# First modulation pieces: five of eight summed by VectorE, and four buffers with three pairs of banks for the rows of x

## The chip, the cores and the metric

One core of one Trainium2 chip. The metric is the device time of one execution in microseconds (us), as the median of several runs. All data are float32 unless said otherwise.

## The reference, cut to what matters

```python
c_act = silu(c)
mod = c_act @ ada_w + ada_b                    # (1, 1024) @ (1024, 6144)
sh1, sc1, g1, sh2, sc2, g2 = split(mod, 6)
h = rms_norm(x, mix_norm_g) * (1 + sc1) + sh1  # x: 512 x 1024
z = h @ w_in                                   # everything else starts from z
...                                            # two attention mixers, then a mixture of 64 experts
```

So the first product with `w_in` needs two things: x, scaled by its row's root and turned so that the 1024 features lie on the partitions, and for every feature its shift `sh1` and scale `sc1`. Those are 2048 of the 6144 columns of `mod`, each a sum over 1024 rows of `ada_w`.

## The kernel before

The 2048 columns are made in eight pieces of 256 columns, numbered 0 to 7. Piece 2p holds shifts and piece 2p+1 scales of the 256 features of pair p. A piece of `ada_w` is 1 MB: 128 partitions by 8 blocks k by 256 columns, in `AF[u]` (`AF[0]` to `AF[5]` in `R_Z`, `AF[6]` and `AF[7]` in `R_WT`). There are two ways to sum one:

- **TensorE** (`ada_quarters`, L1346): eight matrix products, block k against a column of `c_act` in `CQ`, each on a group of 32 rows of the array, so that four partial sums stand in a bank `QBANK[u]`. VectorE copies them to `ACC` (`ada_parts`, L922). Every matmul of float32 is two instructions in the profile, so one piece is 16 of L1346.
- **VectorE** (`ada_sum`, L886 and L888): one multiply and seven multiply-adds over 128 x 256, with partial sums for 128 partitions in `ACC`.

Either way TensorE then turns the partial sums into sums that lie on the partitions (`ada_by_feature`, L1330, two matmuls of one column, four instructions a piece), VectorE adds bias and gain (`mod_columns`, L913 and L915), ScalarE applies them to HT (`modulate`, L708), and TensorE multiplies (`project_first`, L1379).

`QUARTERS = [0, 1, 2, 3, 5, 7]` lists the pieces that TensorE sums; VectorE sums 4 and 6. The first two are summed ahead of the projection. `project_first` runs over k = 0 to 7, and in each k over the four row tiles t. After t = 1 of k = 1, 3, 5 it calls `ada_by_feature` for the two pieces of the next pair; after k = 0, 2, 4 it calls `ada_quarters` for those of the next two pieces that TensorE sums. k needs its half pair to be modulated (`s_hma`) and its quarter of the first weights (`s_w0`).

Ahead of that stand the rows of x. ScalarE makes the root of each of the four row tiles; VectorE scales a tile into `HROW[t % 2]` (`x_row`, L903); TensorE turns it in two halves of four transposes into banks 6 and 7 (`turn_row`, L1314); ScalarE takes bank 6 (L699) and VectorE bank 7 (`take_xt_first`, L907). The single pair of banks makes tile t wait for both copies of tile t-1, and the two buffers make `x_row` wait for transposes.

The work of each engine is written out by hand in one order. SyncE issues all loads in this order: c, gain and bias, constants, four tiles of x, pieces 0 and 1, first quarter of the weights, pieces 2 and 3, second quarter, 4 and 5, third quarter, 6 and 7, fourth quarter, further constants, a 32 KB load, 2 MB of the second weights. None of these waits for work of an engine other than the memsets at the start. Behind them piece 8 waits for seven finished sums (`s_acc`) and piece 9 for eight, since they use the buffers of pieces 6 and 7. ScalarE issues six small loads of 4 to 32 KB (QKG, bfg, rbias) right behind the first pair's `modulate`.

Of the kernel before, what the change touches and what calls it, by code (L numbers as in the profile page):

```python
# [25 lines left out]
P = 128  # L26
# [5 lines left out]
NT = S // P  # L32
# [12 lines left out]
HC = 256  # L45
# [58 lines left out]
    return sum(a in into for into in INTO[:n]) + (a == 0 and n > NM - TAIL)  # L104


QUARTERS = [0, 1, 2, 3, 5, 7]
QBANK = {0: 0, 1: 1, 2: 6, 3: 7, 5: 6, 7: 7}

NEG = -1e30  # L110
NOTOK = 1024.0
# [49 lines left out]
def build(nc, a):  # L161
    f32, i32, bf16 = mybir.dt.float32, mybir.dt.int32, mybir.dt.bfloat16
    ALU, ACT, AX = mybir.AluOpType, mybir.ActivationFunctionType, mybir.AxisListType

    st = contextlib.ExitStack()
    with st:
# [16 lines left out]
        R_G = sb("R_G", [P, 8192])  # L183
# [5 lines left out]
        X = R_XM[:, 0:4096].rearrange("p (t n) -> p t n", t=NT)  # L189
        MOD = R_XM[:, 4096:8192].rearrange("p (r n) -> p r n", r=4)  # L190
        HT = R_HT[:, :].rearrange("p (k s) -> p k s", k=KD)
# [4 lines left out]
        AF = [R_Z[:, 2048 * u:2048 * (u + 1)].rearrange("p (k n) -> p k n", k=KD) for u in range(6)]\  # L196
            + [AD[:, 0], AD[:, 1]]
        ROWS = R_A[0:32, 0:P]
        ACC = R_A[:, :].rearrange("p (b n) -> p b n", b=4)
        HROW = R_S[:, 0:2048].rearrange("p (b n) -> p b n", b=2)  # L200
        JUNK = R_S[:, 2048:3072]
        SQT = R_S[:, 0:2048].rearrange("p (t n) -> p t n", t=NT)
        GN = R_G[:, 0:1024]

# [25 lines left out]
        def tab(at):  # L230
# [22 lines left out]
        ssx = sb("ssx", [P, 12])  # L253
# [8 lines left out]
        CQ = R_S[:, 3072:3072 + 32 * KD].rearrange("p (k h) -> p k h", k=KD)  # L262
# [18 lines left out]
        PS = st.enter_context(nc.psum_tensor("PS", [P, 8, 512], f32))  # L281
# [10 lines left out]
        s_rowst, s_ada1, s_mcol, s_hma, s_htd = map(sem, (  # L292
            "rows_turned", "first_ada_done", "mod_columns_ready", "h_ready_act", "ht_ready_dve"))
# [6 lines left out]
        s_cact, s_acc, s_ones, s_madd, s_mod2 = map(sem, (  # L300
            "c_act_ready", "ada_sums_ready", "ada_spread", "mod_added", "mod2_ready"))
        s_ssx, s_hrow, s_xpose, s_ht = map(sem, ("x_root_ready", "h_row_ready", "h_transposed", "ht_ready"))
# [34 lines left out]
        s_aq = sem("ada_quarters_done")  # L337
# [8 lines left out]
        def need(eng, s, value):  # L346

            if isinstance(value, int) and value <= 0:
                return
            eng.wait_ge(s, value)  # L350
# [331 lines left out]
        def _(act):  # L682
# [13 lines left out]
                               bias=cst[:, C_SC:C_SC + 1]).then_inc(s_ssx, 1)  # L696
            for t in range(NT):
                act.wait_ge(s_xpose, 2 * t + 1)
                act.activation(HT[:, 0:4, P * t:P * t + P], PS[:, 6, :].rearrange("p (k s) -> p k s", k=4), ACT.Copy)\  # L699
                    .then_inc(s_ht, 1)  # L700
            act.sem_inc(s_zfree, 4)
            act.wait_ge(s_ht, NT)
# [91 lines left out]
            for n in range(8):  # L794
                t = n // 2
# [77 lines left out]
        def _(dve):  # L873
            link = Chain(dve, s_dch)

            def ada_sum(u):

                src = AF[u] if u < 8 else AD[:, u % 2]
                acc = ACC[:, u % 4]
                if u < 8:  # L880
                    dve.wait_ge(s_af[u], 16)
                    need(dve, s_ada1, u - 3)
                else:
                    dve.wait_ge(s_ada[u % 2], 16 * (u // 2 - 3))
                    need(dve, s_ones, u - 11)
                link(dve.tensor_scalar(acc, src[:, 0], cact[:, 0:1], None, ALU.mult))  # L886
                for k in range(1, KD):
                    ins = dve.scalar_tensor_tensor(acc, src[:, k], cact[:, k:k + 1], acc, ALU.mult, ALU.add)  # L888
                    if k < KD - 1:
                        link(ins)  # L890
                ins.then_inc(s_acc, 1)
# [6 lines left out]
            def x_row(t):  # L898
                dve.wait_ge(s_ssx, t + 1)
                link(dve.reciprocal(ssx[:, 8 + t:9 + t], ssx[:, 4 + t:5 + t]))  # L900
                if t >= 2:
                    dve.wait_ge(s_xpose, 2 * t - 2)
                dve.tensor_scalar(HROW[:, t % 2], X[:, t, :], ssx[:, 8 + t:9 + t], None, ALU.mult).then_inc(s_hrow, 1)  # L903

            def take_xt_first(t):
                dve.wait_ge(s_xpose, 2 * t + 2)
                dve.tensor_copy(HT[:, 4:8, P * t:P * t + P], PS[:, 7, :].rearrange("p (k s) -> p k s", k=4))\  # L907
                    .then_inc(s_htd, 1)

            def mod_columns(p):  # L910
# [6 lines left out]

            def ada_parts(u):

                dve.wait_ge(s_aq, QUARTERS.index(u) + 1)  # L920
                need(dve, s_ada1, u - 3)
                dve.tensor_copy(ACC[:, u % 4], PS[:, QBANK[u], 0:HC]).then_inc(s_acc, 1)  # L922

            x_row(0)
            x_row(1)
            take_xt_first(0)
            x_row(2)
            take_xt_first(1)
            x_row(3)
            take_xt_first(2)  # L930
            take_xt_first(3)
            for p in range(4):
                for u in (2 * p, 2 * p + 1):
                    if u in QUARTERS:
                        ada_parts(u)
                    else:
                        ada_sum(u)
                mod_columns(p)

            def log_forget():  # L940
# [116 lines left out]
            for n in range(8):  # L1057
                t, cols = n // 2, slice(512 * (n % 2), 512 * (n % 2) + 512)
# [16 lines left out]
            for n in range(8):  # L1075
                t, cols = n // 2, slice(512 * (n % 2), 512 * (n % 2) + 512)
# [220 lines left out]
        def _(pe):  # L1297
# [13 lines left out]
            def turn(dst_bank, src, ready):  # L1311

                for k in range(4):
                    ins = pe.transpose(PS[:, dst_bank, P * k:P * k + P], src[:, P * k:P * k + P], ident)  # L1314
                ins.then_inc(ready, 1)

            def turn_row(t):
                pe.wait_ge(s_hrow, t + 1)
                for half in range(2):
                    need(pe, s_htd if half else s_ht, t)  # L1320
                    turn(6 + half, HROW[:, t % 2, 512 * half:512 * half + 512], s_xpose)

            def ada_by_feature(u):

                p, r = u // 2, u % 2
                pe.wait_ge(s_acc, u + 1)
                need(pe, s_mcol, p - 1)
                for half in range(2):
                    n = 2 * r + half
                    ins = mm(PS[:, 4 + p % 2, n:n + 1], ACC[:, u % 4, P * half:P * half + P], ones[:, 0:1],  # L1330
                             start=True, stop=True)
                ins.then_inc(s_ada1, 1)

            def ada_quarters(u):

                pe.wait_ge(s_cact, 3)
                pe.wait_ge(s_af[u], 16)
                if u == 2:
                    pe.wait_ge(s_ht, NT)
                elif u == 3:  # L1340
                    pe.wait_ge(s_htd, NT)
                elif u > 3:
                    pe.wait_ge(s_acc, QUARTERS[QUARTERS.index(u) - 2] + 1)
                for k in range(KD):
                    g = k % 4
                    ins = mm(PS[32 * g:32 * g + 32, QBANK[u], 0:HC], CQ[:, k, :], AF[u][:, k, :], start=k < 4, stop=k >= 4)  # L1346
                ins.then_inc(s_aq, 1)

            for t in range(NT):
                turn_row(t)  # L1350
            for u in range(2):
                ada_quarters(u)
            for u in range(2):
                ada_by_feature(u)

# [419 lines left out]
```

## Time and profile before

| | |
|---|---|
| median of 3 runs | 1297.62 us (1295.75 to 1299.5) |
| the profiled execution | 1296.77 us, of which the span is 1294.9 us |
| TensorE busy | 1204.2 us, 93% of the span |
| VectorE busy | 462.3 us, 36% |
| mean granted clock of TensorE | 0.971 of full |

A span runs from the first instruction to the last. "Idle before" behind an instruction is the time its engine stood still before it, with the instruction or transfer that ended the wait. "Us to landing" of a load counts from the start of its issue to the arrival of its last byte. The change touches the first 51 us of the span only.

### The profile page before, as it was taken

What the parts mean: (1) busy time and instruction counts of PE and PEld (TensorE: products, weight loads), DVE (VectorE), ACT (ScalarE), POOL (GpSimd) and SP (SyncE); (2) the same over time, 40 slices, a digit from 0 to 9 for tenths busy, and PEclk for the clock granted to TensorE, in tenths of its full rate; (3) what the DMA queues carried; (4) which work ended last, traced back from release to release, by engine and by line L of the source; (5) the groups of instructions that cost most, each with busy time, mean ns of one, the idle gap of its engine ahead of it and who ended that gap; (6) DMA issues with size and microseconds to landing.
All of it is one profiled execution on the core that took longest, in us unless ns stands there. A gap on an engine that the chain in (4) does not pass through costs nothing.

```text
span 1294.9 us, 14018 instructions
## 1 busy us (share of the span) xinstructions
PE 1204.2 (93%) x4705; PEld 605.5 (47%) x4705; DVE 462.3 (36%) x1239; ACT 197.5 (15%) x452; POOL 193.2 (15%) x221
## 2 busy tenths in 40 slices
PE   6999999999999999996999998888999888999985
PEld 3444544444888544443444443333444343444442
DVE  2536557100666232554332333222323222233322
ACT  3210001011655001110010110000101010011100
POOL 0000000000220000100123222221222112213212
PEclk9999999999999999997999999888999899999998
DMA  8966661112000301257499999999989999989972
GB/s 278 369 207 227 221 225 65 65 65 105 27 0 1 130 30 83 91 228 306 170 333 372 387 361 378 367 360 372 366 279 381 385 363 387 384 267 378 360 218 35
DMA packets 87327, 311.51 MB, mean 241 GB/s; under 512 B 12225, under 2 KB 37985, under 8 KB 62049
## 3 DMA queue, kind: packets, MB, share of 16 engines
q1 hardware_dynamic: 71040, 272.77, 54.6%
q0 software_dynamic: 14784, 35.68, 11.8%
q10 hardware_dynamic: 1440, 2.27, 0.5%
q8 instruction: 35, 0.57, 0.2%
q14 instruction: 28, 0.22, 0.0%
HBM read 295.47 MB, written 34.08 MB: 254 GB/s over the span
## 4 chain that ended last, share of the span: by engine, by line
PE 73%; DMA 19%; DVE 2%; issue 2%; SPq 2%; ACT 1%; POOL 0%; DVEq 0%; POOLq 0%; ACTq 0%
PE PS L1396 19%; PE PS L1685 18%; DMA R_WT<-w_up_e 9%; PE PS L1706 9%; PE PS L1564 4%; PE PS L1535 4%; DMA R_XM<-w_up_e 3%; PE PS L1468 2%; PE PS L1379 2%; PE PS L1671 2%; PE PS L1444 2%; DMA out<-second_sum 2%; DMA R_Z<-w_up_e 2%; PE PS L1574 2%; PE PS L1456 1%
## 5 line engine op out<-in xcount | busy, mean ns | idle before, releaser
L1396 PE MATMUL PS<-R_WT,R_HT 128*128 128x512 f32 x576 | 248.2, 592 | 0.0
L1685 PE MATMUL PS<-R_Z,R_G 128*128 128x512 f32 (+1 forms) x496 | 202.6, 629 | 13.4 <-DMA R_Z<-w_up_e 10.1
L1396 PEld LDWEIGHTS PS<-R_WT,R_HT 128*128 128x128 f32 x576 | 109.3, 190 | 135.9 <-issue 135.8
L1232 DVE TENSOR_TENSOR R_G<-R_G,PS 128x256 f32<-128x256 f32 x50 | 30.5, 610 | 368.2 <-ACT R_G L836 368.2
L1685 PE MATMUL PS<-R_WT,R_G 128*64 128x512 f32 (+1 forms) x400 | 143.4, 623 | 17.0 <-DMA R_Z<-w_up_e 12.1
L1685 PEld LDWEIGHTS PS<-R_Z,R_G 128*128 128x128 f32 (+1 forms) x496 | 75.6, 173 | 111.4 <-issue 111.4
L628 POOL DMA_INDIRECT R_G<-h_rows,gidx x54 | 56.2, 1040 | 446.4 <-DVE gidx L1221 367.4
L841 ACT ACTIVATE R_G<-PS 128x256 f32<-128x256 f32 x50 | 19.2, 384 | 571.5 <-PE PS L1693 555.5
L1685 PE MATMUL PS<-R_XM,R_G 128*128 128x512 f32 (+1 forms) x208 | 95.6, 614 | 8.3 <-DMA R_WT<-w_up_e 8.3
L1706 PE MATMUL PS<-R_Z,R_G 128*128 128x512 f32 (+1 forms) x248 | 99.7, 603 | 0.8 <-issue 0.8
L1253 DVE SCALAR_TENSOR_TENSOR R_G<-PS,slx,R_XM 128x512 f32<-128x512 f32 x100 | 75.0, 751 | 61.8 <-PE PS L1706 61.8
L1685 PEld LDWEIGHTS PS<-R_WT,R_G 128*64 128x64 f32 (+1 forms) x400 | 52.1, 161 | 93.4 <-issue 93.4
L634 POOL DMA_INDIRECT out<-R_G,ridx x38 | 55.9, 1470 | 104.4 <-DVE R_G L1253 57.1
L1706 PE MATMUL PS<-R_WT,R_G 128*64 128x512 f32 (+1 forms) x200 | 69.6, 599 | 0.0
L1671 PE MATMUL PS<-cst,R_G 128*128 128x128 f32 x416 | 56.7, 282 | 13.2 <-DMA R_G<-h_rows,gidx 13.2
L1008 DVE CUSTOM_DVE_ANT_0 R_S<-PS,R_A 128x128 f32<-128x128 f32 (+1 forms) x64 | 28.9, 489 | 106.5 <-PE PS L1444 106.4
L888 DVE SCALAR_TENSOR_TENSOR R_A<-R_WT,cact,R_A 128x256 f32<-128x256 f32 x119 | 57.7, 485 | 4.3
L1685 PEld LDWEIGHTS PS<-R_XM,R_G 128*128 128x128 f32 (+1 forms) x208 | 35.0, 170 | 50.0 <-issue 50.0
L1671 PEld LDWEIGHTS PS<-cst,R_G 128*128 128x128 f32 x416 | 49.1, 146 | 14.7 <-DMA R_G<-h_rows,gidx 14.7
L1564 PE MATMUL PS<-R_Z,R_HT 128*128 128x512 f32 x128 | 55.4, 592 | 0.0
L1535 PE MATMUL PS<-R_WT 128*128 128x512 f32 x128 | 55.4, 592 | 0.0
L1706 PEld LDWEIGHTS PS<-R_Z,R_G 128*128 128x128 f32 (+1 forms) x248 | 35.1, 165 | 38.7 <-issue 38.6
(250 smaller groups left out, 1239.1 us busy)
## 6 DMA issues: line engine op xcount, KB each, us to landing
R_Z<-w_gate_e SPq DMA_DIRECT2D x26, 1024.0 KB, 13.9
R_Z<-w_up_e SPq DMA_DIRECT2D x26, 1024.0 KB, 21.8
R_Z<-w_down_e SPq DMA_DIRECT2D x26, 1024.0 KB, 17.0
R_WT<-w_gate_e SPq DMA_DIRECT2D x25, 1024.0 KB, 14.8
R_WT<-w_up_e SPq DMA_DIRECT2D x25, 1024.0 KB, 23.0
R_WT<-w_down_e SPq DMA_DIRECT2D x25, 1024.0 KB, 19.6
R_WT<-ada_w SPq DMA_DIRECT2D x18, 1024.0 KB, 7.5
R_WT<-w_in SPq DMA_DIRECT2D x9, 2048.0 KB, 10.3
```

Source lines behind the costliest of these rows:

```text
L628: pool.indirect_dma_start(out=XG[0:rows(j), b, :], out_offset=None, in_=h2_dram, in_offset=bass.IndirectOffsetOnAxis(ap=gidx[b][0:rows(j), ...
L634: pool.indirect_dma_start(out=sum_dram if n else a["out"], out_offset=bass.IndirectOffsetOnAxis(ap=index[0:part.shape[0], 0:1], axis=0), i ...
L888: ins = dve.scalar_tensor_tensor(acc, src[:, k], cact[:, k:k + 1], acc, ALU.mult, ALU.add)
L1008: ins = dve.tensor_tensor_reduce(out=PB[:, b, at:at + w], in0=PS[:, g, src:src + w], in1=TB[:, b, S - w:S], scale=1.0, scalar=-3e38, op0=A ...
L1232: dve.tensor_tensor(AR[:, b, :].rearrange("p (k d) -> p d k", k=2), by_line(SIL[:, b, :], 2), by_line(PS[:, b, F:2 * F], 2), ALU.mult).the ...
L1253: dve.scalar_tensor_tensor(OB[:, b, 512 * half:512 * half + 512], PS[:, 2 + half, :], slx[:, bass.ds(j % 8, 1), 2:3].rearrange("p o c -> p ...
L1396: ins = mm(PS[:, t, :], HT[:, k, P * t:P * t + P], WR[:, b, k, :], start=k == 0, stop=k == KD - 1)
L1535: ins = mm(PS[:, 2 * half + r, :], YT[:, 4 * r + k, P * t:P * t + P], w[:, k, 512 * half:512 * half + 512], start=k == 0, stop=k == 3)
L1564: ins = mm(PS[:, n % 4, :], MT[:, k, P * t:P * t + P], WO[:, k, 512 * half:512 * half + 512], start=k == 0, stop=k == KD - 1)
L1671: ins = pe.transpose(PS[:, 4 + half, P * k:P * k + P], XG[:, b, 512 * half + P * k:512 * half + P * k + P], ident)
L1685: ins = mm(PS[w * h:w * h + w, b, :].rearrange("p (g n) -> p g n", g=2), XT[:, b, k, w * h:w * h + w], WGU[n][:, k], start=k == 0, stop=k ...
L1706: ins = mm(PS[w * h:w * h + w, 2 + half, :], AT[:, b, k, w * h:w * h + w], WDN[n][:, k, 512 * half:512 * half + 512], start=k == 0, stop=k ...
```

## The change

TensorE sums pieces 0, 1 and 2; VectorE sums 3 to 7. Pieces 0 and 1 share bank 5, in columns 0 to 255 and 256 to 511; piece 2 uses bank 6. The rows of x get four buffers `XROW[t]` and the pairs of banks (6,7), (0,1), (2,3), (6,7). TensorE turns tiles 0 to 2, sums pieces 0 and 1, then turns tile 3, which alone waits for a copy. VectorE sums piece 3 ahead of its copy of piece 2. No load is added, removed or moved in SyncE's order.

```diff
-QUARTERS = [0, 1, 2, 3, 5, 7]
-QBANK = {0: 0, 1: 1, 2: 6, 3: 7, 5: 6, 7: 7}
+QUARTERS = [0, 1, 2]
+QBANK = {0: 5, 1: 5, 2: 6}
+QCOL = {0: 0, 1: HC, 2: 0}
+XBANK = (6, 0, 2, 6)
...
+        XROW = R_G[:, 2048:6144].rearrange("p (b n) -> p b n", b=NT)
...
             def x_row(t):
                 dve.wait_ge(s_ssx, t + 1)
                 link(dve.reciprocal(ssx[:, 8 + t:9 + t], ssx[:, 4 + t:5 + t]))
-                if t >= 2:
-                    dve.wait_ge(s_xpose, 2 * t - 2)
-                dve.tensor_scalar(HROW[:, t % 2], X[:, t, :], ssx[:, 8 + t:9 + t], None, ALU.mult).then_inc(s_hrow, 1)
+                dve.tensor_scalar(XROW[:, t], X[:, t, :], ssx[:, 8 + t:9 + t], None, ALU.mult).then_inc(s_hrow, 1)
...
             def ada_parts(u):
 
-                dve.wait_ge(s_aq, QUARTERS.index(u) + 1)
-                need(dve, s_ada1, u - 3)
-                dve.tensor_copy(ACC[:, u % 4], PS[:, QBANK[u], 0:HC]).then_inc(s_acc, 1)
+                dve.wait_ge(s_aq, max(2, u + 1))
+                dve.tensor_copy(ACC[:, u % 4], PS[:, QBANK[u], QCOL[u]:QCOL[u] + HC]).then_inc(s_acc, 1)
 
             x_row(0)
             x_row(1)
             take_xt_first(0)
             x_row(2)
+            x_row(3)
             take_xt_first(1)
-            x_row(3)
             take_xt_first(2)
+            ada_parts(0)
+            ada_parts(1)
             take_xt_first(3)
-            for p in range(4):
-                for u in (2 * p, 2 * p + 1):
-                    if u in QUARTERS:
-                        ada_parts(u)
-                    else:
-                        ada_sum(u)
+            mod_columns(0)
+            ada_sum(3)
+            ada_parts(2)
+            mod_columns(1)
+            for p in range(2, 4):
+                ada_sum(2 * p)
+                ada_sum(2 * p + 1)
                 mod_columns(p)
...
             def turn_row(t):
                 pe.wait_ge(s_hrow, t + 1)
                 for half in range(2):
-                    need(pe, s_htd if half else s_ht, t)
-                    turn(6 + half, HROW[:, t % 2, 512 * half:512 * half + 512], s_xpose)
+                    if t == 3:
+                        pe.wait_ge(s_htd if half else s_ht, 1)
+                    turn(XBANK[t] + half, XROW[:, t, 512 * half:512 * half + 512], s_xpose)
...
-                pe.wait_ge(s_acc, u + 1)
+                pe.wait_ge(s_acc, 4 if u == 2 else u + 1)
...
-            for t in range(NT):
+            for t in range(3):
                 turn_row(t)
             for u in range(2):
                 ada_quarters(u)
+            turn_row(3)
             for u in range(2):
                 ada_by_feature(u)
```

## Rows read from the trace of the kernel before

**Rows 1.** The page, part 4: shares of the chain that ended last.

```profile
PE 73%; DMA 19%; DVE 2%; issue 2%; SPq 2%; ACT 1%; POOL 0%; DVEq 0%; POOLq 0%; ACTq 0%
```

**Rows 2.** Chain of the first 110 us: start us, us, what.

```profile
18.41 1.86 PE PS L1346 x32
...
28.27 1.86 PE PS L1346 x32
...
32.84 5.26 PE PS L1379 x12
38.09 1.00 PE PS L1346 x16
...
41.01 0.79 PE PS L1330 x8
...
50.75 8.69 PE PS L1379 x20
```

**Rows 3.** Timeline of TensorE, 9 to 30 us: start, us, instructions, idle before.

```profile
13.13 5.28 PE L1314 MATMUL PS<-cst,R_S 128*128 128x128 f32 x24 [1.65 <-DVE R_S L903]
...
22.90 5.37 PE L1379 MATMUL PS<-R_WT,R_HT 128*128 128x512 f32 x8 [1.48 <-ACT R_HT L708]
```

**Rows 4.** Timeline of VectorE: bias and gain of a pair, then sums of pieces 8, 9.

```profile
21.47 0.16 DVE L913 TENSOR_TENSOR mcol<-PS,gcol 128x4 f32<-128x4 f32 x1 [0.70 <-PE PS L1330]
...
56.37 0.35 DVE L886 TENSOR_SCALAR R_A<-R_WT,cact 128x256 f32<-128x256 f32 x1 [5.22 <-DMA R_WT<-ada_w]
...
60.28 0.35 DVE L886 TENSOR_SCALAR R_A<-R_WT,cact 128x256 f32<-128x256 f32 x1
60.67 3.61 DVE L888 SCALAR_TENSOR_TENSOR R_A<-R_WT,cact,R_A 128x256 f32<-128x256 f32 x7
```

**Rows 5.** Timeline of SyncE, issue of pieces 1, 3, 4, 5, 6, 7: start, us.

```profile
5.04 1.35 SPq L460 DMA_DIRECT2D R_Z<-ada_w  x1
...
11.69 2.92 SPq L460 DMA_DIRECT2D R_Z<-ada_w  x1
...
18.18 0.71 SPq L460 DMA_DIRECT2D R_Z<-ada_w  x1
...
18.93 2.92 SPq L460 DMA_DIRECT2D R_Z<-ada_w  x1
...
25.43 2.63 SPq L460 DMA_DIRECT2D R_WT<-ada_w  x1
...
28.11 6.68 SPq L460 DMA_DIRECT2D R_WT<-ada_w  x1
```

**Rows 6.** DMA view at those six issues, same order: KB, us to landing.

```profile
R_Z<-ada_w SPq DMA_DIRECT2D x1, 1024.0 KB, 11.6
...
R_Z<-ada_w SPq DMA_DIRECT2D x1, 1024.0 KB, 12.4
...
R_Z<-ada_w SPq DMA_DIRECT2D x1, 1024.0 KB, 14.0
...
R_Z<-ada_w SPq DMA_DIRECT2D x1, 1024.0 KB, 17.8
...
R_WT<-ada_w SPq DMA_DIRECT2D x1, 1024.0 KB, 16.4
...
R_WT<-ada_w SPq DMA_DIRECT2D x1, 1024.0 KB, 16.7
```

**Rows 7.** DMA view of 27 to 33 us.

```profile
DMA packets 1066, 0.65 MB, mean 109 GB/s; under 512 B 514, under 2 KB 1066, under 8 KB 1066
```

**Rows 8.** Windows: stretch, length, busy (instructions) of PE, PEld, DVE, ACT, POOL; clock; DMA; GB/s.

```profile
24.10:27.50 3.40, 3.40 (x5) 1.35 (x4) 0.00 (x0) 0.00 (x0) 0.00 (x0) 0.51 1.07 327
```

**Rows 9.** Windows of TensorE alone, expert stage: length, busy (instructions), clock, DMA, GB/s.

```profile
640.00:644.00 4.00, 2.95 (x12) 1.00 0.51 205
...
708.00:712.00 4.00, 4.00 (x15) 0.72 1.03 391
```

**Rows 10.** Timeline of TensorE at 706 us.

```profile
706.44 0.69 PE L1685 MATMUL PS<-R_WT,R_G 128*64 128x512 f32 x1 [2.33 <-DMA R_Z<-w_up_e]
```

More of the change, by code:

```diff
@@ L698, in _ @@
                 act.wait_ge(s_xpose, 2 * t + 1)
-                act.activation(HT[:, 0:4, P * t:P * t + P], PS[:, 6, :].rearrange("p (k s) -> p k s", k=4), ACT.Copy)\
+                act.activation(HT[:, 0:4, P * t:P * t + P], PS[:, XBANK[t], :].rearrange("p (k s) -> p k s", k=4), ACT.Copy)\
                     .then_inc(s_ht, 1)
@@ L900, in x_row @@
                 link(dve.reciprocal(ssx[:, 8 + t:9 + t], ssx[:, 4 + t:5 + t]))
-                if t >= 2:
-                    dve.wait_ge(s_xpose, 2 * t - 2)
-                dve.tensor_scalar(HROW[:, t % 2], X[:, t, :], ssx[:, 8 + t:9 + t], None, ALU.mult).then_inc(s_hrow, 1)
+                dve.tensor_scalar(XROW[:, t], X[:, t, :], ssx[:, 8 + t:9 + t], None, ALU.mult).then_inc(s_hrow, 1)
             def take_xt_first(t):
                 dve.wait_ge(s_xpose, 2 * t + 2)
-                dve.tensor_copy(HT[:, 4:8, P * t:P * t + P], PS[:, 7, :].rearrange("p (k s) -> p k s", k=4))\
+                dve.tensor_copy(HT[:, 4:8, P * t:P * t + P], PS[:, XBANK[t] + 1, :].rearrange("p (k s) -> p k s", k=4))\
                     .then_inc(s_htd, 1)
@@ L1339, in ada_quarters @@
                     pe.wait_ge(s_ht, NT)
[L1340 to L1343, printed above, removed]
                 for k in range(KD):
                     g = k % 4
-                    ins = mm(PS[32 * g:32 * g + 32, QBANK[u], 0:HC], CQ[:, k, :], AF[u][:, k, :], start=k < 4, stop=k >= 4)
+                    ins = mm(PS[32 * g:32 * g + 32, QBANK[u], QCOL[u]:QCOL[u] + HC], CQ[:, k, :], AF[u][:, k, :], start=k < 4, stop=k >= 4)
                 ins.then_inc(s_aq, 1)
-            for t in range(NT):
+            for t in range(3):
                 turn_row(t)
```

## The prediction

> **What bounds the kernel now.** I read the page first: the chain that ended last is TensorE for 73% and transfers for 19% [rows 1]. The transfers belong to the experts' weights, long after the changed part, so the question is what stands in the chain of the first 51 us [rows 2]. The reader is to see there that TensorE works without a gap from 22.90 us on, and that three stretches of the partial sums on TensorE are links of it: 1.86 us for pieces 2 and 3, then 1.00 us for piece 5 and the same again for piece 7. Behind 51 us TensorE goes on into the second weights, so a shift of the end of the last columns (50.75 us, where the projection resumes) passes on one to one, and everything up to there can be reckoned as one time. The third view is the timeline of TensorE [rows 3]: 24 transposes of x take 5.28 us with their waits, and the projection starts at 22.90 us after 1.48 us of standing still. The fourth, and the one that decides here, is when the pieces land [rows 5, 6], read as start of the issue plus time to landing:
>
> - piece 1: 5.04 + 11.6 = 16.6 us
> - piece 3: 11.69 + 12.4 = 24.1 us
> - piece 4: 18.18 + 14.0 = 32.2 us
> - piece 5: 18.93 + 17.8 = 36.7 us
> - piece 6: 25.43 + 16.4 = 41.8 us
> - piece 7: 28.11 + 16.7 = 44.8 us
>
> In the kernel before, TensorE took up piece 5 at 38.09 us [rows 2], 1.4 us after it had landed. The stream of loads is therefore almost as late as its users, and SyncE waits for none of them, so no earlier work of an engine makes a piece come sooner. I keep these six times for the changed kernel.
>
> **The front of it.** The transposes before the wait ended at 13.13 - 1.65 = 11.5 us [rows 3]. One tile is 8 of the 24 transposes, 5.28 / 3 = 1.76 us. Tiles 1 and 2 now follow without waiting for copies: 11.5 + 3.5 = 15.0 us. Piece 0 takes half of 1.86 us [rows 2], to 15.95 us; piece 1 waits for its landing at 16.6 us and is done at 17.6 us; tile 3 follows to 19.35 us, and the columns of pieces 0 and 1 take 0.8 us (0.79 us for eight instructions [rows 2]), to 20.2 us. From bias and gain to the projection were 22.90 - 21.47 = 1.43 us [rows 3, 4], so the projection starts at about 21.7 us, 1.2 us earlier. The scalings into four buffers cost what they did; VectorE's work of 1.2 us more ahead of its copies lies beside the transposes. Bounds: 0 if the new waits (tile 3 behind piece 1) cost what the old ones did, 1.5 us if TensorE starts each tile at once.
>
> k = 0 then takes 5.37 us if it meets the low clock as before, to 27.1 us, or 8 x 0.44 = 3.5 us if not (12 instructions took 5.26 us at full clock [rows 2]). Piece 2 adds 0.93 us, the two tiles of k = 1 take four instructions, 1.75 us, and TensorE is at the columns of pieces 2 and 3 at 29.8 us or 27.9 us. VectorE has started piece 3 on its landing at 24.1 us. A sum costs 60.28 - 56.37 = 3.91 us from start to start and 60.67 + 3.61 - 60.28 = 4.00 us by itself [rows 4]: done at 28.1 us, the copy of piece 2 by 28.6 us. So the columns end between 29.4 and 30.6 us, against 32.84 us before [rows 2]. **Up to here the change gains 2.2 to 3.4 us.**
>
> **Where that gain goes.** VectorE has now to sum piece 4, which lands at 32.2 us, and then piece 5, which lands at 36.7 us. The sum of 4 ends at 36.2 us, that of 5 at 36.75 + 4.0 = 40.75 us. Before, piece 5 cost 1.00 us of TensorE's time; now 4.0 us of VectorE's stand between its landing and the columns. TensorE gets there sooner: 12 instructions (5.26 us) and four (1.75 us) behind 29.4 to 30.6 us are 36.4 to 37.6 us, then the columns of piece 4. It stands still for 2.7 to 3.9 us. The columns of piece 5 take 0.4 us (half of 0.79) to 0.6 us behind a wait; I take 0.5: 41.25 us. Before, this point was 41.01 + 0.79 = 41.80 us [rows 2]. Of the gain 0.55 us is left, whatever the front did.
>
> The last pair has the same form. Bias and gain take 0.35 us (two instructions of 0.16 us [rows 4]), to 41.6 us; piece 6 has landed at 41.8 us; two sums are 3.91 + 4.0 us, to 49.8 us; the columns of piece 7 end at 50.3 us. Before, the point was 50.75 us. **Sum on this path: -0.4 us** (bounds -0.3 and -0.7 by the columns' 0.6 or 0.4 us and by what a semaphore costs on the way).
>
> TensorE's own path to that point: from 41.25 us 16 instructions of 0.44 us, 7.0 us, and 0.4 us of the columns of piece 6: 48.7 us, so it waits for 1.1 us more. This is where the clock comes in. Before, it fell after a wait of 1.48 us [rows 3] and stood at 0.51, which is 1.2 instead of 2.4 GHz, from 24.1 to 27.5 us [rows 8]: 1.7 us lost. In the expert stage it fell each of the four times that TensorE had stood still for over 2.1 us, of which one is shown: 2.33 us [rows 10], and 0.72 over a following stretch; after waits of together 1.05 us it stayed at 1.00 [rows 9]. The new wait of 2.7 to 3.9 us is longer than any of these triggers, so I expect the fall behind it. It costs 1.7 us, of which the 1.1 us of waiting cover all but 0.6: the columns of 6 and 7 end at 41.25 + 7.0 + 1.7 + 0.8 = 50.75 us. **With it the sum is 0.0 us.** And then the second wait is gone, and with it a second trigger. If the clock does not fall in this stretch, but behind the wait of 1.1 us, nothing covers it: -0.4 + 1.7 = +1.3 us.
>
> The Trainium skill, "TensorE: Matmul & The Clock Gate", Part 1, says that the place of the clock's changes against the matmuls varies between runs of one and the same kernel. By that page the fall could come in the stretch, behind it or in neither, and the sum would be 0.0, +1.3 or -0.4 us. This trace has one execution and does not show the variation.
>
> **Other edits.** Banks 0 to 3 are used for x, and the projection writes them only after `modulate`, behind all copies. Seven finished sums now come at 45.8 us, where before the sum of piece 6 ended at about 46.1 us, so piece 8 is loaded no later. The eighth comes at 49.8 us instead of 48.5 us, so piece 9 lands about 1.2 us later; its sum before began at 60.28 us [rows 4] only because piece 8's had to end. The cover is TensorE's projection, which needs that sum at some 88 us; without the cover it would cost 1.2 us. ScalarE's six small loads go out 1.2 us earlier, in the midst of pieces 4 and 5.
>
> **The rivals.**
> - *The loads don't come so late.* From 27 to 33 us only 0.65 MB were moved, at 109 GB/s [rows 7]; pieces 6 and 7 land 3.0 us apart, about 350 GB/s [rows 5, 6]. At that rate the stretch would take 1.9 us, so 4.1 us are lost in it. For: small packets are half of it, and the small loads move. Against: they are still there, and in the same order behind the first `modulate`. If the stretch were whole, piece 5 would land at 32.6 us, VectorE would sum back to back from 30.9 us at the latest, and the end would come at 48.6 us: -2.1 us, or -3.4 us with the clock full in k = 0.
> - *TensorE is the bound after all*: the removed 0.93 + 1.00 + 1.00 us, the front's 1.2 us and the 1.7 us of low clock all count, -5.8 us. Against it stands that a pair on VectorE is 0.35 + 7.9 + 0.5 = 8.8 us, where TensorE's period before was 50.75 - 41.80 = 8.95 us.
> - *Piece 5 lands later*, since the small loads now compete with it from an earlier time. It is slower than before once piece 5 lands past 37.1 us, and each us costs 1 us; a slow stretch twice as long (4.1 us) gives +3.7 us, or +4.1 us with the clock falling. For: the piece has no slack at all now, where it had 1.4 us. Against: what an engine has to move ahead of the piece's last byte is the same bytes in either kernel, since the last small load had landed ahead of 36.7 us.
> - *The clock falls behind the second wait*: +1.3 us.
>
> **How the numbers follow.** The forecast (VectorE behind the landing of piece 5; the clock falls between the waits or not at all, 0.0 to -0.4 us) gets 0.5, the fall behind the second wait 0.17, the earlier landings 0.15, TensorE as bound 0.04, the later landing 0.14. The likeliest time is 1296.77 + 0.0 us in the profiled execution, which lies 0.9 us under the median of the runs; added to the median, **1297.6 us**. The time of a measurement of this kernel can be told from no change by 0.3%, 3.9 us. Only TensorE as bound is wholly past that on the fast side, with a little of the earlier landings (0.05 together), and about a third of the later landing on the slow side (0.05); the rest, 0.90, is within. The range goes from the earlier landings' far end, -3.4 us, to nearly the later landing's +3.7 us: 1294.2 to 1301.0 us. The likeliest case by itself, with the spread of the runs before of some 1.9 us, is 1295.5 to 1299.5 us.
>
> **What would show it.** The first instruction of k = 0 at about 21.7 us; idle time of TensorE of some 3 us ahead of the columns near 41 us, ended by VectorE's L888; VectorE waiting for `ada_w` transfers ahead of the sums of pieces 3, 4 and 5, to 24.1, 32.2 and 36.7 us; the projection resuming at 50.3 to 50.8 us. The prediction is wrong if piece 5 lands more than 1 us away from 36.7 us, if a sum takes other than 4.0 us beside the busy ScalarE, or if the granted clock falls more than once between 41 and 55 us.

## The result, and the profile after

The changed kernel takes 1302.41 us (median of 8 runs, 1300.22 to 1304.88), the kernel before in the same comparison 1298.47 us (8 runs, 1295.75 to 1301.41). The ratio is 1.0033 with a 95% interval of 1.0019 to 1.0048: slower, where no change was forecast, and 1.4 us above the range. The profiled execution has a span of 1301.3 us against 1294.9 us, 6.4 us more.

The page of the changed kernel (busy us, share of the span, instructions; then the chain that ended last):

```profile
PE 1206.5 (93%) x4657; PEld 608.9 (47%) x4657; DVE 471.7 (36%) x1260; ACT 197.9 (15%) x452; POOL 193.2 (15%) x221
...
PE 72%; DMA 20%; SPq 3%; DVE 3%; issue 2%; ACT 0%; POOL 0%; DVEq 0%; POOLq 0%; ACTq 0%
```

TensorE has 48 instructions less, three pieces of 16, and is yet 2.3 us longer busy. A busy time that grows while work is taken away is the first hint of its clock.

The part that was changed goes through the steps that the prediction names. Timeline of the changed kernel, VectorE and TensorE (start, us, instructions, idle before):

```profile
21.85 3.67 PE L1380 MATMUL PS<-R_WT,R_HT 128*128 128x512 f32 x8 [1.47 <-ACT R_HT L711]
...
24.76 0.35 DVE L889 TENSOR_SCALAR R_A<-R_Z,cact 128x256 f32<-128x256 f32 x1 [3.99 <-DMA R_Z<-ada_w]
...
32.88 0.35 DVE L889 TENSOR_SCALAR R_A<-R_Z,cact 128x256 f32<-128x256 f32 x1 [2.29 <-DMA R_Z<-ada_w]
...
36.80 0.35 DVE L889 TENSOR_SCALAR R_A<-R_Z,cact 128x256 f32<-128x256 f32 x1
...
40.84 0.71 PE L1334 MATMUL PS<-cst,R_A 128*128 128x1 f32 x4 [3.30 <-DVE R_A L891]
```

Its chain (start, us, what):

```profile
18.54 14.32 DMA R_Z<-ada_w
...
40.84 0.71 PE PS L1334 x4
41.55 8.56 PE PS L1380 x16
50.12 0.79 PE PS L1334 x8
50.90 8.69 PE PS L1380 x20
59.59 27.47 PE PS L1397 x64
```

The projection starts 1.05 us earlier than at [rows 3]; VectorE waits for pieces 3 and 4. It does not wait for piece 5, which had landed at 36.68 us when the sum of piece 4 ended at 36.80 us: the chain starts from the load of piece 4, issued at 18.54 us, and goes through two sums, 7.9 us. TensorE stands still for 3.30 us until VectorE has summed piece 5; then 16 instructions take 8.56 us, since the clock has fallen:

```profile
41.20:44.60 3.40, 3.40 (x7) 1.70 (x7) 2.80 (x8) 1.52 (x2) 0.00 (x0) 0.50 1.07 347
```

That is the windows view: 0.50 of full clock for 3.40 us. The projection resumes at 50.90 us, 0.15 us later than the 50.75 us of [rows 2]. So of the 6.4 us between these two spans, 0.15 us are in the changed part. The rest comes later. The chains there, changed kernel first:

```profile
426.87 27.55 PE PS L1536 x64
...
687.40 22.26 DMA R_Z<-w_up_e
...
1079.77 26.11 DMA R_WT<-w_up_e
...
1216.50 1.42 POOL out L637
```

and the kernel before:

```profile
425.13 27.47 PE PS L1535 x64
...
684.89 21.30 DMA R_Z<-w_up_e
...
1074.18 28.00 DMA R_WT<-w_up_e
...
1210.80 1.42 POOL out L634
```

The distance is 1.7 us at 425 us, 3.5 us at the end of the wait at 706 us (687.40 + 22.26 against 684.89 + 21.30), 3.7 us at 1102 us and 5.7 us at 1210 us. None of this code was changed. TensorE alone in windows (length, busy, clock, DMA, GB/s), changed kernel, then before:

```profile
422.00:426.00 4.00, 3.41 (x20) 0.69 0.00 0
...
590.00:602.00 12.00, 12.00 (x40) 0.57 0.98 398
```

```profile
422.00:426.00 4.00, 3.41 (x25) 1.00 0.00 0
...
590.00:602.00 12.00, 10.33 (x39) 0.72 1.01 425
```

The same work, 0.15 us apart, with the same busy share of 3.41 us in 4, has full clock in one execution and 0.69 in the other, which loses 1.6 us there (1.7 us of distance less the 0.15 us). At 590 to 602 us both have low clock, the changed kernel more of it. Whether that belongs to the change or to the two executions is what the runs had to tell.

### The profile page after: what moved, and what is told of

Its sections match the earlier page's. It is cut to its first block, busy times and chain, and to the rows that moved or that the text cites. A ratio compares the mean times of both kernels' runs of the same rounds, so it can differ in the third digit from the quotient of the medians.

```text
span 1301.3 us, 13936 instructions
## 1 busy us (share of the span) xinstructions
PE 1206.5 (93%) x4657; PEld 608.9 (47%) x4657; DVE 471.7 (36%) x1260; ACT 197.9 (15%) x452; POOL 193.2 (15%) x221
## 4 chain that ended last, share of the span: by engine, by line
PE 72%; DMA 20%; SPq 3%; DVE 3%; issue 2%; ACT 0%; POOL 0%; DVEq 0%; POOLq 0%; ACTq 0%
PE PS L1397 19%; PE PS L1686 18%; DMA R_WT<-w_up_e 9%; PE PS L1707 9%; PE PS L1536 4%; PE PS L1565 4%; DMA R_XM<-w_up_e 3%; PE PS L1469 2%; PE PS L1672 2%; PE PS L1445 2%; DMA out<-second_sum 2%; DMA R_Z<-w_up_e 2%; PE PS L1575 2%; PE PS L1380 1%; PE PS L1457 1%
## 5 line engine op out<-in xcount | busy, mean ns | idle before, releaser
L1686 PE MATMUL PS<-R_WT,R_G 128*64 128x512 f32 (+1 forms) x400 | 147.0, 638 | 21.2 <-DMA R_Z<-w_up_e 16.3
L637 POOL DMA_INDIRECT out<-R_G,ridx x38 | 55.9, 1470 | 105.9 <-DVE R_G L1256 58.4
L1707 PE MATMUL PS<-R_WT,R_G 128*64 128x512 f32 (+1 forms) x200 | 69.6, 599 | 0.0
L891 DVE SCALAR_TENSOR_TENSOR R_A<-R_WT,cact,R_A 128x256 f32<-128x256 f32 x126 | 61.1, 485 | 4.5
L1672 PEld LDWEIGHTS PS<-cst,R_G 128*128 128x128 f32 x416 | 49.1, 146 | 14.4 <-DMA R_G<-h_rows,gidx 14.4
```

What stands on the lines that cost most here:

```text
L637: pool.indirect_dma_start(out=sum_dram if n else a["out"], out_offset=bass.IndirectOffsetOnAxis(ap=index[0:part.shape[0], 0:1], axis=0), i ...
L1672: ins = pe.transpose(PS[:, 4 + half, P * k:P * k + P], XG[:, b, 512 * half + P * k:512 * half + P * k + P], ident)
L1686: ins = mm(PS[w * h:w * h + w, b, :].rearrange("p (g n) -> p g n", g=2), XT[:, b, k, w * h:w * h + w], WGU[n][:, k], start=k == 0, stop=k ...
L1707: ins = mm(PS[w * h:w * h + w, 2 + half, :], AT[:, b, k, w * h:w * h + w], WDN[n][:, k, 512 * half:512 * half + 512], start=k == 0, stop=k ...
```

## The experiments

Three groups of four kernels were timed, each group on one chip. Each timed kernel has 12 executions, with 35 of the kernel before beside each group, and one trace. Six more executions, e5 to e8, e17 and e18, were made for their traces alone. Executions of one kernel differ by 1.2 to 2.7 us (standard deviation), so a mean of 12 is known to about 0.7 us (standard error, as for all means below).

| run | median, us | ratio to before | interval |
|---|---|---|---|
| e1, before + 0.15 us | 1298.35 | 1.0006 | 0.9991 to 1.0021 |
| e2, VectorE's sums alone | 1302.89 | 1.0028 | 1.0010 to 1.0045 |
| e3, the front alone | 1297.54 | 0.9991 | 0.9978 to 1.0005 |
| e4, front, pieces 5 and 7 by TensorE | 1299.75 | 1.0005 | 0.9992 to 1.0019 |
| e9, before, wait filled | 1297.64 | 0.9997 | 0.9986 to 1.0009 |
| e10, changed, waits filled | 1300.86 | 1.0013 | 0.9994 to 1.0033 |
| e11, front alone, wait filled | 1297.67 | 1.0001 | 0.9988 to 1.0015 |
| e12, e9 + 1.3 us | 1300.40 | 1.0016 | 1.0003 to 1.0030 |
| e13, changed, small loads late | 1297.66 | 0.9995 | 0.9978 to 1.0012 |
| e14, before, small loads late | 1297.37 | 0.9994 | 0.9978 to 1.0010 |
| e15, e10 with small loads late | 1299.11 | 1.0003 | 0.9987 to 1.0019 |
| e16, e11 with small loads late | 1296.16 | 0.9981 | 0.9963 to 0.9998 |

**e1: is a shift of 0.15 us enough?**

```diff
             project_first()
+            for _ in range(1):
+                mm(PS[:, 5, 0:96], ones, cst[:, 0:96], start=True, stop=True)
             project(0, 1)
```

> The kernel before with one extra matmul of 96 columns into an unused bank between the first and the second projection, and nothing else: the work behind 59 us starts some 0.15 us later, as it does in the changed kernel. Theory A (the changed kernel loses its time behind 51 us because the same work, 0.15 us later, meets the clock of TensorE otherwise; the clock changes at times that are fixed from the start of the span): the ratio to before is 1.002 to 1.004, low clock shows near 423.5 us, and TensorE's table products near 590 us run at the low clock from their start. Theory B (the loss behind 51 us has to do with what the change moved: buffers, banks, loads): +0.15 us, ratio 1.000, no low clock at 423 us.

1.0006, where theory A gave 1.002 to 1.004; the interval just reaches 1.0021. There is a low clock neither at 24 us nor at 423 us in this trace, and the last columns end at 49.46 us. The second projection starts at 58.34 us, 1.3 us earlier than in the changed kernel, so this one trace can't test what a start 0.15 us later does at 423 us. But it shows that the clock does not change at fixed times of the span, as theory A has it: the kernel before has two courses in its front, with the low clock of [rows 8] and without.

**e2: VectorE's sums alone.**

```diff
-QUARTERS = [0, 1, 2, 3, 5, 7]
-QBANK = {0: 0, 1: 1, 2: 6, 3: 7, 5: 6, 7: 7}
+QUARTERS = [0, 1, 2]
+QBANK = {0: 0, 1: 1, 2: 6}
...
+            ada_parts(0)
+            ada_parts(1)
+            mod_columns(0)
+            ada_sum(3)
+            ada_parts(2)
+            mod_columns(1)
+            for p in range(2, 4):
+                ada_sum(2 * p)
+                ada_sum(2 * p + 1)
+                mod_columns(p)
```

> Pieces 3 to 7 by VectorE, the rows of x as before (one pair of banks, two buffers). Both theories: the projection resumes between 50.3 and 51.0 us, since piece 5 lands at 36.7 us whatever the front does. Theory A: the rest hangs on that time alone; at 50.9 us as in the changed kernel the ratio is 1.003, at another time it may be anything from 0.999 to 1.004. Theory B, loss from VectorE's sums: 1.003 wherever it resumes; loss from the buffers and banks: 1.000.

1.0028, nearly the whole effect. Its chain has the landing of piece 5 in it, then the start of the second projection:

```profile
18.70 17.97 DMA R_Z<-ada_w
...
58.93 27.47 PE PS L1399 x64
```

Piece 5 landed at 36.67 us, after the sum of piece 4 had ended. It is the order, not the front, that is exposed to it. But this trace starts the second projection only 0.2 us behind the mean of the kernel before (58.7 us, below), while the mean of the 12 executions is 3.5 us more than that of the kernel before: most of the loss does not show at 59 us.

**e3: the front alone.**

```diff
-QUARTERS = [0, 1, 2]
-QBANK = {0: 5, 1: 5, 2: 6}
-QCOL = {0: 0, 1: HC, 2: 0}
+QUARTERS = [0, 1, 2, 3, 5, 7]
+QBANK = {0: 5, 1: 5, 2: 6, 3: 7, 5: 6, 7: 7}
+QCOL = {0: 0, 1: HC, 2: 0, 3: 0, 5: 0, 7: 0}
```

(on the changed kernel, with the order of VectorE's copies and TensorE's waits of the kernel before)

> Four buffers, three pairs of banks and the new order of the rows of x; TensorE sums pieces 0, 1, 2, 3, 5, 7 as before. My steps: the projection starts 1.1 us earlier, and what is gained stays up to piece 5's landing at 36.7 us, so it resumes at 49.3 to 50.0 us instead of 50.75 us (48 us if the low clock at 24 us goes too). Theory A: ratio 0.997 to 1.001 by the clock behind. Theory B, loss from buffers and banks: 1.003.

0.9991: buffers and banks cost nothing that 12 executions can tell. In this trace the projection began at 20.92 us, met the low clock at once, and TensorE then stood 1.29 us ahead of piece 5, whose landing was 37.30 us; the second projection started at 58.81 us.

**e4: pieces 5 and 7 back to TensorE.**

```diff
-QUARTERS = [0, 1, 2]
-QBANK = {0: 5, 1: 5, 2: 6}
-QCOL = {0: 0, 1: HC, 2: 0}
+QUARTERS = [0, 1, 2, 5, 7]
+QBANK = {0: 5, 1: 5, 2: 6, 5: 7, 7: 6}
+QCOL = {0: 0, 1: HC, 2: 0, 5: 0, 7: 0}
...
             for p in range(2, 4):
                 ada_sum(2 * p)
-                ada_sum(2 * p + 1)
+                ada_parts(2 * p + 1)
                 mod_columns(p)
```

> The new front, pieces 3, 4 and 6 by VectorE, pieces 0, 1, 2, 5 and 7 by TensorE: only piece 3's 0.93 us go from TensorE, and the two pieces that land last of their pair keep the quick way. My steps: TensorE takes piece 5 at 36.8 us on its landing, the columns end at 40.2 us, the last ones at 49.1 us, 1.7 us earlier than before. Theory A: ratio 0.996 to 1.001, by the clock behind. Theory B (VectorE's sums cost later): between 1.000 and 1.003.

1.0005, no gain. In its trace TensorE stood still for 1.77 us ahead of piece 5, and then the clock fell: four instructions of the projection took 3.57 us instead of 1.91 us. In this execution that eats the gain of coming earlier: TensorE waits for the load instead, and pays for the wait. The projection resumed at 50.55 us, not at the 49.1 us expected.

**e5 to e8: two more traces of each kernel.** e5 and e6 are the changed kernel, e7 and e8 the kernel before, unchanged.

> The changed kernel unchanged, for a second trace. Theory A2 (the change makes TensorE meet the low clock at 423 us, in the attention's end, in nearly every execution): low clock near 420 to 427 us again. Theory C (where the clock falls in that stretch is chance, and the three traces that have it, all with VectorE's sums, have it by chance): present or not, with the chance of about a half.

> The same once more, for a third trace. Theory A2: low clock near 423 us again. Theory C: as likely not.

> The kernel before unchanged, for a second trace. Theory A2: full clock from 60 to 580 us, as in its first trace. Theory C: low clock at the attention's end in one of two.

> The same once more, for a third trace. Theory A2: full clock from 60 to 580 us. Theory C: low clock there in one of two.

No trace of the four has low clock between 60 and 580 us. Low clock at 419 to 427 us is in the first trace of the changed kernel, in e2, e4 and later e13, and in none of the other four traces of the changed kernel. So theory A2 is refuted, and the 1.6 us lost there in the first trace are no part of what the change costs every time. That the place is pure chance, theory C, is not shown: of the ten traces of kernels in which VectorE sums three pieces or more, four have it, of the ten others none. The starts of the second projection are the other yield. Chains of the kernel before, e7 and e8:

```profile
57.96 27.47 PE PS L1396 x64
...
58.73 27.47 PE PS L1396 x64
```

with 59.44 us in its first trace (50.75 + 8.69 [rows 2]): 58.7 us on the average of three. Chains of the changed kernel, e5 and e6:

```profile
58.42 27.47 PE PS L1397 x64
...
60.60 27.47 PE PS L1397 x64
```

TensorE of the two extremes in windows, first e6 (changed), then e7 (before):

```profile
40.00:47.00 7.00, 6.64 (x11) 0.51 1.08 355
```

```profile
22.00:28.00 6.00, 4.88 (x32) 1.00 1.07 342
```

In e6 the low clock lasted 6.8 us behind the wait for VectorE, twice what I had reckoned with, and cost 3.2 us. In e5, which had met the low clock ahead of the projection, at 21.8 us, the wait of 2.73 us for VectorE was followed by none. In e7 the wait of 1.48 us ahead of the projection was followed by no low clock at all.

**e9 to e12: the clock taken out of the front.** Extra matmuls, whose result is not used, fill TensorE's waits.

```diff
+            def fill(n):
+                for _ in range(n):
+                    mm(PS[:, 7, 0:256], ones, cst[:, 0:256], start=True, stop=True)
...
             def project_first():
+                pe.wait_ge(s_htd, NT)
+                fill(3)
...
                             ada_by_feature(k + 1)
+                            fill({1: 0, 3: 7, 5: 2}[k])
                             ada_by_feature(k + 2)
```

The line with `[k]` is in e10 alone (and later in e15). e12 has three more such matmuls in bank 5 between the two projections.

> The kernel before, with three extra matmuls of 256 columns (about 1.3 us, their result unused) in TensorE's wait of 1.48 us ahead of the projection, so that it has no wait left there. Theory C (the clock): no low clock ahead of 60 us in any execution, the projection resumes at 49.1 to 49.3 us always; before it was 49.3 to 50.8 us in three traces, so -0.5 to -1.0 us or ratio 0.9992 to 0.9996 by itself. Theory D (the loss is in what VectorE's sums or the buffers do to later stages): 1.000.

> The changed kernel with extra matmuls in all three waits of the front: three ahead of the projection, seven ahead of the columns of piece 5, two ahead of those of piece 7. Theory C: no low clock ahead of 60 us, the projection resumes at 50.0 to 50.8 us always, and what is left against the filled kernel before is the 1.0 to 1.5 us of the resumption: ratio to before 1.0000 to 1.0008. Theory D: the loss stays, 1.0025 to 1.003.

> The new front with the old division of the pieces (as in the run of the front alone) and three extra matmuls ahead of the projection. Theory C: resumes at 48.4 to 49.9 us by the landing of piece 5, 1 us ahead of the kernel before on average: 0.9985 to 0.9992. Theory D: as the front alone, 0.999.

> The filled kernel before with three more extra matmuls, 1.3 us, between the first and the second projection: VectorE's sums, buffers and banks as before, but everything behind starts as late as in the filled changed kernel. If a later start is all that counts, it is slower than the filled kernel before by 1.3 us (0.0010) and equal to the filled changed kernel within 0.0006. If a later start is worth more than itself, it shows here; if only VectorE's sums cost more (theory D), it is 1.3 us slower than the filled kernel before and 2 to 3 us faster than the filled changed kernel.

None of the four traces has low clock ahead of 60 us. Extra work of some 1.3 us made the kernel before 1.0 us faster (mean of 12: 1298.0 against 1299.0 us), as theory C gives, though within what 12 executions can tell. The filled changed kernel has 1301.0 us, 3.0 us more than e9; the filled kernel before with 1.3 us of delay has 1300.4 us, 2.4 us more than e9. Second projections of e10 and e12:

```profile
60.39 27.47 PE PS L1404 x64
```

```profile
58.76 27.47 PE PS L1402 x64
```

e9's started at 57.70 us. In e10 piece 4 landed at 34.2 us, 2 us later than at [rows 5, 6], and two sums in a row followed it, so it started 2.7 us later than e9: that is nearly all of its 3.0 us. Theory D, a cost of VectorE's sums in later stages, has no support between these two: what a later start costs, e10 costs. e11 has 1.0001, a little worse than expected; its second projection starts at 57.60 us, 0.1 us ahead of e9's, since TensorE stands 1.08 us for piece 5.

**e13 to e16: the landing of the pieces.** ScalarE's six small loads (QKG, bfg, rbias) go out behind the last `modulate` instead of the first.

```diff
             modulate(0)
+            for p in range(1, 4):
+                modulate(p)
             for n, g in enumerate(("qn_a", "qn_b", "kn_a", "kn_b")):
...
-            for p in range(1, 4):
-                modulate(p)
```

> The changed kernel with ScalarE's six small loads issued behind the last modulate (some 51 us) instead of the first. If it is these loads that make the slow stretch of 27 to 33 us, pieces 4 to 7 land up to 4 us earlier (piece 5 at 32.6 us), and the second projection starts at 57 to 58 us instead of 58.4 to 60.6 us, bound by VectorE's sums alone: 1.9 to 3 us faster than the changed kernel, ratio to before 1.0000 to 1.0015. If the slow stretch stays, the landing of piece 5 stays at 35.7 to 36.7 us and the ratio near 1.003.

> The kernel before with the same edit. It does not wait for the pieces, so only the clock and chance move it: 0.9995 to 1.0005. If it gains as much as the changed kernel does, the landing of the pieces is not what the edit acts through.

> The changed kernel with extra matmuls in its waits and the small loads late: both suspected costs taken away. The second projection starts at 57 to 58 us in every execution with the clock full; 0.9985 to 0.9995, 3.5 to 5 us faster than the changed kernel. If VectorE's sums cost something else in later stages, it stays above 1.001.

> The new front, the old division of the pieces, three extra matmuls ahead of the projection, small loads late: the candidate for the best version. TensorE never waits for a piece; the second projection starts at 56.9 to 57.3 us, 1.5 us ahead of the kernel before: 0.9980 to 0.9990.

The DMA view of 27 to 33 us in e13, against the 0.65 MB of [rows 7]:

```profile
DMA packets 1854, 2.14 MB, mean 356 GB/s; under 512 B 38, under 2 KB 1597, under 8 KB 1853
```

The slow stretch is gone from here; e13 has one at 55 to 57 us instead, of 139 GB/s, behind all eight pieces. And pieces 4 to 7 land at 27.9, 32.2, 36.6 and 39.6 us, up to 5 us earlier. VectorE and TensorE of e13:

```profile
33.20 0.35 DVE L889 TENSOR_SCALAR R_A<-R_Z,cact 128x256 f32<-128x256 f32 x1
...
37.25 0.61 PE L1334 MATMUL PS<-cst,R_A 128*128 128x1 f32 x4 [0.97 <-DVE R_A L891]
...
46.14 0.61 PE L1334 MATMUL PS<-cst,R_A 128*128 128x1 f32 x4 [0.96 <-DVE R_A L891]
```

Now VectorE sums pieces 4 and 5 back to back, TensorE's wait is 0.97 us instead of 3.30 us, and the second projection starts here:

```profile
55.43 27.47 PE PS L1397 x64
```

That is 4.1 us ahead of the mean of the changed kernel's five traces, 59.5 us. Its time is 1298.2 us (mean of 12) against 1302.5 us in the changed kernel's eight runs, 4.3 us less, or 3.5 us less than all twelve executions of it. The kernel before, e14, gains 0.9 us by the same edit (1298.1 against 1298.9 us), not clear of its uncertainty. So the edit acts through the wait of VectorE's sums for their pieces. e15 shows that filling has its price when the wait is short: seven matmuls of 0.45 us are longer than the wait that is left, its second projection starts at 57.65 us, and it is no faster than e13, where 3.5 to 5 us under the changed kernel had been expected. e16 starts at 56.11 us with TensorE summing as before, and is the fastest kernel of the study: 0.9981, faster than before by its interval, and some 5 us under the changed kernel's mean.

**e17 and e18: the changed kernel twice more.**

> The changed kernel once more for a trace. In three traces the second projection started at 58.4, 59.6 and 60.6 us, and 1.7, 1.7 and 3.2 us of matmul time were lost to low clock ahead of it. If the front carries the loss, the start is at 60 us or later and the mean of the five lies 1.5 us or more above that of the kernel before (58.7 us); if the loss is behind it, the start is at 58.4 to 59.6 us and the rest of the span is 1240 us or more, against 1235.5 to 1240.7 us in the traces of before.

> The same for a fifth trace: a start at 60 us or later if the front carries the loss; at 58.4 to 59.6 us, and 1240 us or more of span behind it, if the loss is behind.

```profile
59.28 27.47 PE PS L1397 x64
...
59.58 27.47 PE PS L1397 x64
```

The five starts of the changed kernel have a mean of 59.5 us, 0.8 us more than the three of before. The span behind them was 1241.7, 1240.0, 1242.0, 1234.6 and 1238.1 us (mean 1239.3), in the kernel before 1235.5, 1240.7 and 1238.4 us (mean 1238.2). So neither expectation came true: the starts of e17 and e18 are under 60 us, and the rest is under 1240 us in both. e17 refutes that the rest is longer every time: its span of 1293.9 us is shorter than that of the first trace of before, with the same change in it.

## Why the prediction was wrong

**What held.** The steps of the front were right within 0.7 us: projection at 21.85 us (21.7 forecast), sum of piece 4 begun at 32.88 us (32.2) and ended at 36.8 us (36.2), TensorE standing still 3.30 us (2.7 to 3.9), the columns of piece 5 done at 41.55 us (41.25), clock low from 41.2 us on, projection resumed at 50.90 us (50.75). Piece 9, forecast 1.2 us later, was not: it landed at 57.6 to 58.6 us in the five traces and at 57.7 to 59.4 us in the three of before. That two sums back to back and the landing of pieces 4 and 5 take all of the gain is shown by e2 and, from the other side, by e13.

**The step that failed** is the base: "the wait of 1.48 us" is followed by low clock "from 24.1 to 27.5 us", and "with it the sum is 0.0 us". I set the changed kernel against an execution of before that had paid 1.7 us for low clock. It doesn't always: e7 and e1 have none, and resume at 49.27 and 49.46 us. The mean start of the three traces of before is 58.7 us, 0.7 us ahead of the execution that I summed against, and the changed kernel's is 59.5 us. The term was +0.8 us, not 0.0 (five traces against three, known to about 0.5 us).

**A term missed** is the low clock's length and number behind the new wait. I gave it 1.7 us, once, with 1.1 us of cover. The five traces lost 1.7, 1.7, 3.2, 1.7 and 3.4 us of matmul time ahead of 60 us; before lost 1.7, 0 and 1.7 us. In e18 the clock fell twice, at 22.0 and at 42.5 us. My reading of the trigger was too strong as well. I wrote that in the expert stage the clock fell each of four times behind a wait of over 2.1 us. That trace has eleven such waits there, and around the one of 3.42 us that ends at 1046.75 us the clock stays full (1.00 from 1042 to 1050 us).

**A rival underpriced** is the later landing of a piece. I gave it 0.14 and thought of piece 5 alone. With the small loads at their old place, piece 4 lands at 30.0 to 34.3 us in the traces. In all five traces of the changed kernel it lands at 32.3 to 32.9 us, and VectorE ends its sum at 36.2 to 36.8 us, after piece 5 has landed (35.7 to 36.7 us). So the path runs from piece 4 through two sums, as in e10, and not from piece 5 through one, as I had it. I had argued only that small loads 1 us earlier would not delay piece 5; that the landing of piece 4 differs by 4 us between executions, one trace could not show. The opposite rival has a slip in its sum: its own terms, 30.9 + 7.9 + 0.5 + 0.35 + 7.9 + 0.5 us, give 48.1 us and -2.7 us, not 48.6 us and -2.1 us.

**The range** rested on three runs of before, within 1.9 us of their median. The 113 executions of before in the comparisons have a standard deviation of 2.3 us and reach from 1294.1 to 1306.9 us. In the three traces of before the start of the second projection differs by 1.5 us and the span behind it by 5.2 us, so most of that spread comes from the stages behind the change.

**The size.** All twelve executions of the changed kernel, the four single ones with them, have a mean of 1301.7 us, the kernel before 1299.0 us: 2.7 us, known to 0.7 us. (The eight of the first comparison alone are 4.1 us above its eight of before.) Of it 0.8 us are seen in the traces at 59 us. The whole spans behind it can't be told apart (1239.3 and 1238.2 us, each known to over 1 us), but a point halfway can. TensorE's wait for the first rows of the experts ends here, first in the kernel before, then in the changed one:

```profile
610.70 1.97 PE L1671 MATMUL PS<-cst,R_G 128*128 128x128 f32 x8 [5.90 <-DMA R_G<-h_rows,gidx]
```

```profile
614.07 1.97 PE L1672 MATMUL PS<-cst,R_G 128*128 128x128 f32 x8 [5.78 <-DMA R_G<-h_rows,gidx]
```

On average this point is at 612.5 us in the five traces of the changed kernel and at 610.7 us in the three of before, 1.8 us apart (known to 0.8 us), and the span behind it is 686.3 us in both (each known to about 1 us). So what the traces show of the loss lies ahead of 611 us: 0.8 us up to 59 us, 0.3 us from the low clock at 423 us, which one of the five had, and 0.9 us between 588 and 600 us, less 0.2 us behind that. At 588 to 600 us the low clock lasted 10.2 us in three of the five and 6.8 us in the other two and in all three of before. The mean granted clock of each execution says the same for more of them: 0.9677 over the twelve of the changed kernel and 0.9700 over the 105 of before beside the groups, which is 3.1 us more of clock time lost (known to 0.8 us), though not all of that is on the path. e2 has 0.9676, but e10 and e15, with the waits filled, have 0.9702 and 0.9703. So more low clock, ahead of 60 us and behind it, goes with VectorE's sums where their waits are not filled. Why it should come behind 60 us is open: e3, e11 and e16 have 10.2 us of it at 590 us too and are no slower than before.

The remaining 0.9 us of the 2.7 us are not seen in the traces. The starts of single executions reach from 58.4 to 60.6 us, so part may be starts that no trace caught; e12, where 1.3 us of pure delay measured 2.4 us with an uncertainty of 0.8 us, leaves room for the view that a delay costs more than itself later on. Neither is shown.

The Trainium skill, "TensorE: Matmul & The Clock Gate", Part 1, says that the place of the clock's changes against the matmuls varies between runs of one and the same kernel. The traces of before agree: behind the same wait of 1.48 us the clock fell at 24.2 us, at 22.7 us and not at all. The traces of the changed kernel add a case of 3.2 us that I had not priced.

## What to carry to other kernels

Before moving work to an idle engine, look at when its input lands: a quick engine that comes late has slack for the load, a slow one that starts on the landing puts its whole duration on the path. Here 1.0 us of TensorE behind the landing of piece 5 became two sums of VectorE, 7.9 us, behind the landing of piece 4, and TensorE's saved time became a wait that also cost it clock. The remedy was at the loads: six small ones moved away from the stream put the changed kernel's second projection 4.1 us earlier, more than the 2.2 to 3.4 us that the change gains ahead of its wait.

For a change of a few us, take several traces of the kernel before as well: the execution that the sum is made against may be a slow or a fast course of the very stretch that is changed.

## What the runs showed of the hardware

- Six loads of 4 to 32 KB, 164 KB together, issued by ScalarE into the stream of SyncE's large loads, held all traffic down to 109 GB/s for 6 us [rows 7]; with them moved behind the pieces the same stretch had 356 GB/s (e13). Their own bytes would take 0.5 us at that rate.
- The clock of TensorE fell or not behind one and the same wait of 1.48 us in different executions (0.51 at 24 us in the first trace of before, 1.00 in e7), and in e6, behind the wait of 3.30 us, it was at half for 6.8 us in a row, while TensorE was busy again.
- At 423 us the same instructions at the same busy share ran once at full clock and once at 0.69 over 4 us, 0.15 us apart, and 1.6 us were lost there.
- Three matmuls of no use, 1.4 us in e9, in a wait of 1.48 us cost nothing that 12 executions can tell (0.9997), and the clock stayed full ahead of 60 us in each of the six traces that had them. Of the 14 traces without them, ten had low clock there.
